# Stage hand-over by halves of 128 tokens in a two-model fp32 kernel on one core, with products of both input parts in one matmul

## The reference

```
def swiglu(h, w_gu, w_down):
    gu = h @ w_gu                      # 1024 x 2*2816
    return (silu(gu[:, :D_FF]) * gu[:, D_FF:]) @ w_down
```

## Time and profile before

| what | value |
|---|---|
| median of 3 runs | 1230.1 us (1229.35 to 1230.11) |
| profiled execution, its own time | 1230.18 us |
| its span, first to last instruction | 1228.5 us |
| mean granted TensorE clock | 0.981 |
| TensorE matmul busy | 1174.2 us (96%) |
| TensorE weight load busy | 1077.2 us (88%) |
| DVE, ACT, POOL busy | 812.7, 559.5, 115.0 us |
| HBM read | 240.90 MB, 197 GB/s over the span |

### The profile page before, as it was taken

The page is one execution under the profiler, slowest core; times in us unless marked ns, Lnnn a source line. Parts: engine busy times, 40 slices in busy tenths (PEclk is TensorE's granted clock), DMA queues, the critical chain, the costliest instruction groups (busy, mean ns, idle before and its releaser), DMA issues.

```text
span 1228.5 us, 20207 instructions
## 1 busy us (share of the span) xinstructions
PE 1174.2 (96%) x8020; PEld 1077.2 (88%) x8020; DVE 812.7 (66%) x1040; ACT 559.5 (46%) x650; POOL 115.0 (9%) x99
## 2 busy tenths in 40 slices
PE   5999999999899999999969999999999998999997
PEld 4887999999787799999969999988989997999996
DVE  6486867777857586777785677766467477444444
ACT  4483543343457354334344434335695435433432
POOL 3300700000330070000010000000000000000000
PEclk8999999999999999999979999998999999999999
DMA  9612477775361257777535666754424543555540
GB/s 365 225 69 103 174 266 296 275 288 206 124 220 70 103 182 266 287 278 293 201 134 213 242 254 265 291 191 161 168 82 149 194 154 149 201 182 176 199 171 35
DMA packets 34852, 242.68 MB, mean 198 GB/s; under 512 B 3793, under 2 KB 5217, under 8 KB 8177
## 3 DMA queue, kind: packets, MB, share of 16 engines
q1 hardware_dynamic: 27792, 196.03, 43.1%
q0 software_dynamic: 5520, 45.17, 10.0%
q10 hardware_dynamic: 1488, 0.76, 0.2%
HBM read 240.90 MB, written 1.05 MB: 197 GB/s over the span
## 4 chain that ended last, share of the span: by engine, by line
PE 79%; DVE 10%; ACT 5%; issue 4%; DMA 1%; SPq 0%; POOL 0%; DVEq 0%; ACTq 0%
PE bank L418 74%; ACT w_hi L802 2%; DVE x_lo L1187 1%; PE bank L493 1%; DVE w_lo L1114 1%; DVE work L1230 1%; PE bank L581 1%; DVE small L1130 1%; DMA raw<-stream 1%; DVE h L1143 1%; DVE x_hi L1185 1%; DVE h L1163 1%; DVE z L1159 1%; PE bank L558 1%; PE bank L571 1%
## 5 line engine op out<-in xcount | busy, mean ns | idle before, releaser
L1114 DVE TENSOR_TENSOR w_lo<-raw,w_hi 128x2048 fp32r<-128x2048 f32 x184 | 431.9, 2354 | 225.8 <-ACT w_hi L802 225.7
L418 PE MATMUL bank<-x_hi,w_hi 128*128 128x256 f32 x1824 | 519.5, 285 | 4.7 <-DVE w_lo L1114 2.3
L418 PE MATMUL bank<-x_lo,w_hi 128*128 128x256 f32 x1824 | 516.1, 283 | 0.0
L418 PE MATMUL bank<-x_hi,w_lo 128*128 128x256 f32 x1824 | 516.0, 283 | 0.0
L802 ACT ACTIVATE w_hi<-raw 128x2048 fp32r<-128x2048 f32 x184 | 350.8, 1908 | 181.3 <-PE bank L418 175.9
L418 PEld LDWEIGHTS bank<-x_hi,w_hi 128*128 128x128 f32 x1824 | 349.7, 192 | 11.2 <-issue 4.8
L418 PEld LDWEIGHTS bank<-x_lo,w_hi 128*128 128x128 f32 x1824 | 349.9, 192 | 1.8
L418 PEld LDWEIGHTS bank<-x_hi,w_lo 128*128 128x128 f32 x1824 | 349.9, 192 | 0.0
L418 PE MATMUL bank<-w_hi,hid_hi 128*128 128x512 f32 x352 | 139.3, 396 | 2.1 <-DVE hid_lo L1218 2.1
L418 PE MATMUL bank<-w_lo,hid_hi 128*128 128x512 f32 x352 | 139.0, 395 | 0.0
L418 PE MATMUL bank<-w_hi,hid_lo 128*128 128x512 f32 x352 | 139.0, 395 | 0.0
(11 more groups left out here) (162 smaller groups left out, 1124.7 us busy)
## 6 DMA issues: line engine op xcount, KB each, us to landing
raw<-stream SPq DMA_DIRECT2D x184, 1024.0 KB, 4.8
work<-ada POOLq DMA_DIRECT2D x24, 1536.0 KB, 7.6
gain_rows<-rows POOLq DMA_DIRECT2D x11, 512.0 KB, 6.4
gate_rows<-rows POOLq DMA_DIRECT2D x3, 512.0 KB, 10.9
h<-x SPq DMA_DIRECT2D x4, 256.0 KB, 5.0
out<-z SPq DMA_DIRECT2D x4, 256.0 KB, 2.1
c<-consts SPq DMA_DIRECT2D x1, 962.0 KB, 13.0
wf<-w_f ACTq DMA_DIRECT2D x2, 256.0 KB, 12.6
```

Of the source, the lines that this page charges most:

```text
L418: last = nc.tensor.matmul(out, stationary, moving, start=start and i == 0, stop=stop and i == 2, skip_group_check=True)
L1114: nc.vector.tensor_tensor(w_lo[j % SLOTS][:, :], raw[j % SLOTS][:, :], w_hi[j % SLOTS][:, :].bitcast(F32), ALU.subtract).then_inc(lo_ready, 1)
```

## The change

1. Both parts of an input tile lie side by side (`x_parts`, `mix_parts`). In FFN gate and up chunks one matmul of 512 columns multiplies `w_hi` with `[x_hi | x_lo]`, and one of 256 columns `w_lo` with `x_hi`: two matmuls with two weight loads for each place (`split_projection`) instead of three. The result lies in two parts of a bank; gate uses banks 0 and 1 (`GATE`), up 2 and 3 (`UP`). ACT copies the second part out (`gate_rest_out`, `up_rest_out`), DVE adds the first (`gate_summed`, and in `after_up`).
2. Stages hand over 128 tokens (m = 0, then m = 1). The last bank products are reordered so that banks 0 and 1 are complete first; `transposes(n, 0)` stand behind the last bank's products. The first gate and up chunks of an FFN are done in halves of 128 tokens (`half_projection`: matmuls of 256 and of 128 columns), with `transposes(n, 1)` between the halves; V likewise (`token_projection`, matmuls of 512 columns as before).
3. For n = 1 to 3 the layer norm with its gain and bias is finished on DVE in two instructions a quarter (`layer_rows`) and `h` itself is transposed; ACT takes `x_hi` and DVE `x_lo` straight from the transposed bank (`input_high`, `input_low`). POOL's `residual_stream` goes. For n = 0, 5, 6, 7 ACT applies gain and shift in instructions of 128 x 128 (`input_full`).
4. The partition sums of the modulation move: `sum_shifts`, now 32 fp32r matmuls of two columns, into the middle of the tail's up chunk, `sum_gates` into the middle of the last two down chunks. Both wait for splits of `ada_acc`, which ACT and DVE do in the tail.
5. At the start half of x and half of the first chunk are loaded first.

```
+            def split_projection(t, j, pair, ks=range(KT)):
+                pe.wait_ge(lo_ready, 3 * t + (j + 1))
...
+                for k in ks:
+                    for n in range(2):
+                        cols = slice(n * P, (n + 1) * P)
+                        nc.tensor.matmul(pair[:, n, :], wh[:, k, cols], x_parts[:, k, :, :].rearrange("p a n -> p (a n)"),
+                                         start=k == 0, stop=False, skip_group_check=True)
+                        last = nc.tensor.matmul(pair[:, n, 0:S], wl[:, k, cols], x_hi[:, k, :], start=False,
+                                                stop=k == KT - 1, skip_group_check=True)
...
+            def half_projection(t, j, pair, n_in, m):
...
+                        both = pair[:, n, :].rearrange("p (a n) -> p a n", a=2)[:, :, tokens(m)]
+                        nc.tensor.matmul(both, wh[:, k, cols], x_parts[:, k, :, tokens(m)], start=m == 0 and k == 0,
+                                         stop=False, skip_group_check=True)
+                        last = nc.tensor.matmul(pair[:, n, tokens(m)], wl[:, k, cols], x_hi[:, k, tokens(m)],
+                                                start=False, stop=k == KT - 1, skip_group_check=True)
...
+            def token_projection(t, j, n_in):
+                token_rows(t, j, B[0], 0, n_in, 0)
+                token_rows(t, j + 1, B[0], 1, n_in, 0)
+                transposes(n_in, 1)
+                token_rows(t, j, B[1], 0, n_in, 1)
+                token_rows(t, j + 1, B[1], 1, n_in, 1)
...
@@ TensorE, ffn @@
+                half_projection(t, j, GATE, n_in, 0)
+                half_projection(t, j + 1, UP, n_in, 0)
+                transposes(n_in, 1)
+                half_projection(t, j, GATE, n_in, 1)
+                half_projection(t, j + 1, UP, n_in, 1)
...
+                if with_ada:
+                    pe.wait_ge(gate_ready, FT * f + FT - 1)
+                    split_projection(t + (FT - 3), j + 5, GATE)
+                    pe.wait_ge(up_ready, FT * f + FT - 1)
+                    split_projection(t + (FT - 3), j + 6, UP, ks=range(0, 4))
+                    sum_shifts(f)
+                    split_projection(t + (FT - 3), j + 6, UP, ks=range(4, KT))
...
+                residual_banks(before_last, (0, 1), hid_hi, hid_lo, 0)
                 if with_ada:
                     sum_gates(f)
...
+                pe.wait_ge(hid_ready, FT * f + FT)
+                pe.wait_ge(lo_ready, 3 * t + (last + 1))
+                residual_banks(last, (0,), hid_hi2, hid_lo2, 0, stop=True).then_inc(res_bank, 1)
+                residual_banks(last, (1,), hid_hi2, hid_lo2, 0, stop=True).then_inc(res_bank, 1)
+                residual_banks(before_last, (2, 3) if with_ada else (3,), hid_hi, hid_lo, 0).then_inc(chunk_done, 1)
+                residual_banks(last, (2,), hid_hi2, hid_lo2, 0, stop=True).then_inc(res_bank, 1)
+                residual_banks(last, (3,), hid_hi2, hid_lo2, 0, stop=True).then_inc(chunk_done, 1)
+                if n_out in (2, 6):
+                    transposes(n_out, 0)
+
+            def sum_shifts(f):
+                pe.wait_ge(ones_ready, 1)
+                pe.wait_ge(acc_ready, 2 * f + 1)
+                pe.wait_ge(gate_ready, FT * f + FT)
+                for q in range(SHIFT_SCALE):
+                    for i in range(2):
+                        at = (i * SHIFT_SCALE + q) * P
+                        last = nc.tensor.matmul(B[0][:, 2 * q:2 * q + 2], mix_flat[:, at:at + P], ones_r[:, 0:2],
+                                                start=q == 0 and i == 0, stop=i == 1, skip_group_check=True)
...
@@ ScalarE, tail @@
                     act.wait_ge(ada_step, KT * ADA_STEPS * (f + 1))
+                    nc.scalar.activation(mix_flat[:, 0:SHIFT_SCALE * P], ada_acc[:, 0:SHIFT_SCALE * P], ACT.Copy)\
+                        .then_inc(acc_hi_ready, 1)
+                gate_rest_out(t, j + 5)
                 split(t, j + 8)
+                silu(FT * f + (FT - 1))
+                if with_ada:
+                    act.wait_ge(acc_shifted, f + 1)
+                    act.wait_ge(shifts_reduced, f + 1)
+                    nc.scalar.activation(mix_flat[:, 0:KT * P], ada_acc[:, SHIFT_SCALE * P:], ACT.Copy)\
+                        .then_inc(acc_hi_ready, 1)
+                up_rest_out(t, j + 5, FT * f + (FT - 1))
                 if not final:
                     split(t, j + 9)
+                hidden_hi(FT * f + (FT - 1), hid_hi2)
...
@@ VectorE, tail @@
+                gate_summed(FT * f + (FT - 1))
                 split(t, j + 8)
                 if with_ada:
+                    dve.wait_ge(acc_hi_ready, 2 * f + 1)
+                    nc.vector.tensor_tensor(mix_flat[:, SHIFT_SCALE * P:2 * SHIFT_SCALE * P],
+                                            ada_acc[:, 0:SHIFT_SCALE * P],
+                                            mix_flat[:, 0:SHIFT_SCALE * P].bitcast(F32), ALU.subtract)\
+                        .then_inc(acc_ready, 1)
+                    dve.wait_ge(gate_rows_landed, 48)
+                    row = ada_acc[0:1, SHIFT_SCALE * P:]
+                    nc.vector.tensor_tensor(row, row, gate_rows[0:1, f, :], ALU.add).then_inc(acc_shifted, 1)
+                    keep_shifts(f)
...
+                after_up(FT * f + (FT - 1))
                 hidden_lo(FT * f + (FT - 1), hid_hi2, hid_lo2)
...
@@ VectorE, n = 2; n = 1 and 3 alike @@
+                    layer_residual(n, 0, chunks)
+                    layer_residual(n, 1, chunks)
+                    layer_rows(n, 0)
+                    layer_residual(n, 2, chunks)
+                    input_low(n, 0)
+                    split(t, 1)
+                    layer_residual(n, 3, chunks)
+                    layer_rows(n, 1)
+                    input_low(n, 1)
```

More of the change, by code:

```diff
@@ L453, in token_projection, with residual_product @@
                 last.then_inc(chunk_done, 1)
-            def to_residual(t, j, xh, xl, tiles, first, last_chunk, before=lambda k: None, rows=range(2)):
-                pe.wait_ge(lo_ready, 3 * t + (j + 1))
+            def residual_product(j, b, tile, xh, xl, k, start=False, stop=False):
                 wh, wl = chunk(w_hi, j % SLOTS, 2), chunk(w_lo, j % SLOTS, 2)
[L461 to L468, removed]
-                    for i in range(2):
[L470 to L480, removed]
-                    last.then_inc(chunk_done, 1)
@@ L483, in input_tile @@
[L483 to L496, removed]
@@ new lines, in residual_product, with residual_banks, input_tile @@
+                return passes(RES[b][:, :], wh[:, tile, cols], wl[:, tile, cols], xh[:, k, tokens(m)],
+                              xl[:, k, tokens(m)], True, start, stop)
+            def residual_banks(j, banks, xh, xl, first_tile, start=False, stop=False):
+                for b in banks:
+                    for i in range(2):
+                        last = residual_product(j, b, i, xh, xl, first_tile + i, start and i == 0, stop and i == 1)
+                return last
+            def input_tile(n, k, m):
+                pe.wait_ge(x_ready, 4 * back(n) + 2 * m + k // 4 + 1)
@@ L539, in sum_shifts @@
[L539 to L544 removed]
+                else:
+                    residual_banks(before_last, (2,), hid_hi, hid_lo, 0)
+                pe.wait_ge(hid_ready, FT * f + FT)
+                pe.wait_ge(lo_ready, 3 * t + (last + 1))
@@ L546, in _ @@
+            def sum_gates(f):
+                pe.wait_ge(acc_ready, 2 * f + 2)
+                pe.wait_ge(ada_kept, f + 1)
+                for c in range(2):
+                    for i in range(2):
+                        at = (2 * i + c) * HALF
+                        last = nc.tensor.matmul(B[c][:, :], ones_r[:, :], mix_flat[:, at:at + HALF], start=i == 0,
+                                                stop=i == 1)
+                last.then_inc(gates_reduced, 1)
             pe.wait_ge(ident_landed, 16)
@@ new lines, in input_full @@
+            def input_full(n, m, gain, shift):
+                for c in range(2):
+                    act.wait_ge(transposed, 4 * back(n) + 2 * m + c + 1)
+                    if m == 1:
+                        act.wait_ge(x_ready, 4 * back(n) + c + 1)
+                    for k in range(4):
+                        cols = slice(k * P, (k + 1) * P)
+                        last = nc.scalar.activation(x_full[:, c, cols], XT[2 * m + c][:, cols], ACT.Identity,
+                                                    bias=shift(4 * c + k), scale=gain(4 * c + k))
+                    last.then_inc(x_full_ready, 1)
```

667 lines of the change are left out of this document (414 added, 253 removed).

## The result

The changed kernel takes 1277.5 us (median of 4 runs, 1275.56 to 1279.83) beside 1230.1 us for the kernel before on the same chip (4 runs, 1229.35 to 1231.48): ratio 1.0385, 95% interval 1.0364 to 1.0405. It is slower, as predicted, and 20 us above the predicted 1257, inside the range. The profiled execution took 1275.56 us with a span of 1273.9, which is 45.4 over the one before, where the sum of the prediction said 27.2.

The account below looks back on a forecast made before the run. TensorE was taken as the bound (79% of the chain), with hand-overs set by DVE's chain. Against 1230.18 us, -11.5 merged products, +39.7 tails, +5.0 clock and -6.0 hand-overs gave +27.2, 1257.4 us; range 1234 to 1284.

Parts of the forecast that it names:

- three tails, with the clock: Ends of the first three FFNs: +39.7 us for stall and sums, +5.0 for half clock behind the standstills.
- merged products outside them, and n = 1, 3, 7: Merging gains 11.5 us; hand-overs into three FFNs, with half products, change by +1.2, +0.3 and +3.6.
- n = 2, 5, 6: Hand-overs into attention 1, an FFN and the mixer: -5.6, -2.5 and -1.7 us.
- start and end: Hand-overs n = 0 and 8: between -4 and +2 us, taken as -1.3.
- The stall: Up chunk of three tails: TensorE waits 10.4 us each for `acc_ready`; no-stall rival 1221 us, chance 0.10.
- The sums: In three tails, behind the wait: 32 shift sums at 0.113 us each, 3.6 us.
- The clock's return: Behind each of three tail standstills, half clock costs 1.65 us, +5.0 in all; other bound nothing.
- Merged products: FFN gate and up chunks: a place goes from 0.36 to 0.35 us, 11.5 us gained.
- The floor of 0.33: Rival in gate and up chunks: a merged place costs 0.33 us, 23 us more gained, 1234; chance 0.10.
- 128-column products: Half products in the first gate and up chunks of each FFN: 0.115 us each, 15.0 for 11.5 a stage.
- The rival of an fp32 price under 256 columns: Half products in first FFN chunks cost 0.22 us each, 27 us more, 1284; chance 0.12.
- Hand-overs: Between stages, from the residual's end to the end of the first products: -6.0 us in all.

Follow-up runs that it names:

- late sums: Changed kernel with all modulation sums moved between banks 1 and 2 of the last down chunk, their splits after the hidden parts: 1240.4 us, ratio 1.0087.
- a kernel with merged products: Kernel before with only the 512-column products over both input parts in all gate and up chunks; sums and hand-overs unchanged: 1222.8 us, ratio 0.9946.
- the 1212.2 with all of them: Kernel before with merged gate and up products, both modulation sums behind the last down chunk, hidden parts finished before the gate split: 1212.2 us, ratio 0.9859.

## Why the prediction was right in direction and 20 us short

Its terms against the two profiled executions (the measured ones are rounded):

| term | predicted | measured |
|---|---|---|
| three tails, with the clock | +44.7 | +54.5 |
| merged products outside them, and n = 1, 3, 7 | -6.4 | -2.8 |
| n = 2, 5, 6 | -9.8 | -8.6 |
| attention, two layers | 0 | +2.9 |
| start and end | -1.3 | -0.7 |
| sum | +27.2 | +45.4 |

- **The stall: right, in place, cause and size.** Three waits of 10.1 us for the low part of `acc`, forecast as 10.4, with the ladder as laid out: the sums began at 18.7 against 18.8. The experiments confirm that it is the loss: without the sums 1222, with the wait out of the up chunk 1240.
- **The sums: the term of the prediction that was mis-sized.** "32 shift sums at 0.113, 3.6" was the price at the full clock, read from the earlier trace rows. They follow a standstill that drops the clock, and took 6.8 us; the late sums show 3.63 for the same instructions at 1.00. That is 3.2 x 3 = 9.7 us, nearly all that the tails were off by.
- **The clock's return: right mechanism, too short in the first tail.** I carried 1.65 us over from the earlier trace rows, where full-width work followed the standstill. Here the clock stayed at 0.50 under the sums, and the eight places behind them then lost another 2.45 us in the first tail, 1.7 and 1.5 in the others. The sums aren't the reason for the 2.45: with two of them in place of 32 the places lost 2.4, 1.7 and 1.4. Why the first tail took longer stays open.
- **Merged products: too high by about a third.** I took 0.36 to 0.35; measured 0.360 to 0.353. The two-digit starts of the earlier trace rows can't give the difference of two prices; the distance of many starts, the 16.88 of a step against 17.1, can. The floor of 0.33 is excluded: the place took 0.353, and undoing the merge cost 10.6 us, not 35.
- **128-column products: right sum, wrong parts.** The forecast of 0.12 + 0.115 = 0.235 a pair was measured as 0.17 + 0.06 = 0.23. The rival of an fp32 price under 256 columns is excluded. The Trainium skill's 81 ns for such a product (TensorE: Matmul & The Clock Gate, Back-to-back issue gap) is above this 0.06, which stands behind a 256-column product of 0.17; no run here has such products in a row, so it isn't contradicted.
- **Hand-overs: n = 2 within 0.1 (-5.5 for -5.6), n = 5 -1.6 for -2.5, n = 6 -1.5 for -1.7.** ACT's instructions on 128 x 128 are spaced 0.36 (eight in 2.90 us), estimated 0.39.
- **Attention: not in the prediction.** TensorE waits 0.6 us in each layer for DVE's `mix_parts` (line 1598: 1.2, 2 times), which fits the new order, in which banks 0 and 1 are completed first and need that part earlier; layer 1 also has a stretch at half clock (0.52 from 403 to 410). What is left of the 2.9 isn't settled, and no experiment was made on it.

The prediction had the hand-overs at -6.0 against the kernel before; they came to about -4, and the attention's +2.9 takes most of that back. What it didn't ask is whether the hand-over by halves gains at all beside a kernel with merged products. By the table it doesn't: +0.4 us over all of it, with 4.2 lost at n = 7, 1.9 at n = 1 and 3 and 0.6 up to attention 0, and 6.4 gained at n = 2, 5 and 6; late sums in both kernels give 1233.8 - 1210.7 = 23.1 us of span against the halves (28.2 by the medians), of which 3 x 6.0 is the sums on the path and their clock. The halves don't win without them either: the changed kernel with no sums at all took 1222.4, 10 us more than the 1212.2 with all of them (5.4 of the 10 are its tails, with their waits for `hid_lo`). The wait that halves remove was the cover of the sums. Whether the sums would fit into the waits that the halves leave (24.2 us for `x_parts` in the three rows of the result) no run tries.

## What to carry to other kernels

An idle stretch on the critical engine may already pay for something: before shortening it, list what runs under it, for that work has to go somewhere, and here it cost more than the shortening gave. Put work that hangs on a long ladder of other engines behind everything that doesn't, not in the middle of a chunk whose results others wait for. And cost an instruction by the clock it will find: behind the standstills of 10 us here all of TensorE's work ran at half speed until the clock was back, and the tiny matmuls there were paid twice.

## What the runs showed of the hardware that was not expected

- 32 fp32r matmuls of two columns took 3.63 us at a granted clock of 1.00 and 6.96 at 0.50: their price nearly doubles at half the clock, though they stream hardly anything.
- The clock stayed at 0.50 through 6.8 us of such matmuls behind a standstill, and in the kernel with late sums it fell behind them without any idle time: 1.00, then 0.94 and 0.64 in its windows, TensorE busy in all three.
- A 128-column product behind a 256-column one with a strided output cost 0.06 us to the next start, and the one ahead of it 0.17 instead of the 0.12 of an ordinary 256-column product. The pair is 0.23, for 384 columns; a merged place has 768 in 0.353. The half product is so dear that 64 of these pairs cost 3.5 us more than 32 whole places.
